# Convolution taps and six modulation pieces in the first projection, eight late pieces on GpSimd in the even attention

## What is computed

```python
mod_l = silu(c) @ w_ada[layer] + b_ada[layer]          # 6 * 1024 values; mod_c the same from c_ctx
sh1, sc1, g1, sh2, sc2, g2 = split(mod_l, 6)
h = rms_norm(x, g) * (1 + sc1) + sh1
qa, ka, va, qk_b, vb, ob, gates = split_cols(h @ w_in)
qk_b = silu(centred_conv(qk_b, conv_w, conv_b))        # 3 taps along the tokens, zero at the ends
mixed = concat([attention(qa, ka, va), mlstm_both_ways(qk_b, vb, gates) * sigmoid(ob)]) @ w_out
x = x + g1 * mixed
f = rms_norm(x, g) * (1 + sc2) + sh2                   # goes to the router and the experts
```

## Time and profile before

| | |
|---|---|
| median of the runs | 3173.81 us |
| span of the profiled execution | 3171.6 us |
| busy: PE, DVE, ACT, POOL | 2890.9, 1441.7, 1113.2, 597.7 us |
| HBM read, written | 576.73 MB, 81.66 MB |

### The profile page before, as it was taken

How to read it: one execution, slowest core, us unless ns; L and a number is a source line. 1 busy time by engine, 2 the same in 40 slices (tenths; PEclk the granted TensorE clock), 3 DMA queues, 4 the chain that set the end, 5 groups by cost and what they waited for, 6 DMA issues and landing times. The chain is left out here.

```text
span 3171.6 us, 72552 instructions
## 1 busy us (share of the span) xinstructions
PE 2890.9 (91%) x27907; PEld 1926.7 (61%) x27907; DVE 1441.7 (45%) x3981; ACT 1113.2 (35%) x2484; POOL 597.7 (19%) x825
## 2 busy tenths in 40 slices
PE   6999988899999879999996999899999959998895
PEld 3666655745544547998673455477776536775573
DVE  2333327855547642232223677666665443222223
ACT  1111114466634313333332444355553203332232
POOL 0000003500038423332230100000002003332233
...
GB/s 344 224 27 26 13 128 283 116 1 1 1 168 212 137 378 414 411 417 416 418 405 154 92 81 72 74 1 1 1 1 103 153 229 364 417 416 417 418 417 300
DMA packets 163276, 654.45 MB, mean 206 GB/s; under 512 B 24204, under 2 KB 36760, under 8 KB 113892
## 3 DMA queue, kind: packets, MB, share of 16 engines
...
HBM read 576.73 MB, written 81.66 MB: 208 GB/s over the span
## 5 line engine op out<-in xcount | busy, mean ns | idle before, releaser
L2724 PE MATMUL ps_g<-w_ring,work 128*32 128x256 f32 x7328 | 435.3, 383 | 26.1 <-DMA w_ring<-in_w 15.2
L2811 DVE STREAM_TRANSPOSE work<-work 128x256 f32<-128x256 f32 x189 | 123.5, 653 | 658.7 <-PE ps_g L2724 630.1
L2724 PEld LDWEIGHTS ps_g<-w_ring,work 128*32 128x32 f32 x7328 | 298.7, 111 | 132.0 <-issue 34.6
L2777 ACT COPY work<-ps_y 32x256 f32<-32x256 f32 x760 | 276.4, 364 | 286.1 <-PE ps_y L2739 276.9
L2724 PE MATMUL ps_g<-w_early,work 128*32 128x256 f32 x4640 | 281.0, 387 | 33.1 <-DMA w_early<-in_w 19.3
L1849 PE MATMUL of_ps_r<-w_early,cat 128*128 128x512 f32 (+1 forms) x608 | 254.9, 575 | 1.6 <-ACT cat L1931 1.6
L2724 PEld LDWEIGHTS ps_g<-w_early,work 128*32 128x32 f32 x4640 | 188.7, 112 | 103.9 <-issue 40.6
L447 PE MATMUL ps_r<-w,hT 128*128 128x512 f32 (+1 forms) x640 | 249.4, 546 | 1.5 <-ACT hT L506 1.5
L2672 POOL DMA_INDIRECT work<-f_dram,ex_idx x200 | 205.1, 1025 | 170.1 <-POOL ex_idx L2669 167.6
L2771 ACT ACTIVATE work<-ps_g 128x128 f32<-128x128 f32 x192 | 53.4, 278 | 512.4 <-PE ps_g L2724 505.8
L2739 PE MATMUL ps_y<-w_ring,work 128*32 128x256 f32 x3680 | 228.4, 382 | 3.4 <-ACT work L2777 3.4
...
## 6 DMA issues: line engine op xcount, KB each, us to landing
...
w_early<-in_w SPq DMA_DIRECT2D x152, 1024.0 KB
...
f_dram<-mo_f SPq DMA_DIRECT2D x18, 512.0 KB, 2.9
...
```

The costliest lines, as they stand in the source:

```text
L2724: mm = pe.matmul(ps_h[rows, :], xT[:, k * UNIT:(k + 1) * UNIT], w[:, :, kk * DE + n * P:kk * DE + (n + 1) * P], start=k == 0, stop=k == KD ...
L2777: w = act.copy(y[b * UNIT:(b + 1) * UNIT, n * 256:(n + 1) * 256], ps_y[n * UNIT:(n + 1) * UNIT, :])
L2811: dve.transpose(xT.rearrange("p (k t) -> p k t", k=KD), xs.rearrange("p (r k) -> p k r", k=KD)).then_inc(x_turned, 1)
```

## The change

Nothing that is computed changes; the work moves between stages.

- The taps are scaled in `modulation`. In the projection ScalarE writes each channel block as middle tap plus bias, straight from PSUM, and VectorE adds the two side taps from PSUM. The first and last column of each tile are kept raw in `L.edges`; at the start of the mLSTM four small additions join the tiles. The mLSTM's `middle` and `convolve` go.
- Six pieces (4 to 9, `SUMMED`) are worked off in tiles 1 to 6 of the projection: SyncE loads half a piece (four blocks of 128x512) at a time into the end of `zT`, which later tiles fill, VectorE multiplies and accumulates for both vectors into the end of `qT`, and SyncE stores the 128x1024 sums to `sum_dram`. In the mLSTM's front twelve loads become eight: six whole pieces, and the sums as one unit of 2 MB (four pieces) and one of 1 MB (two), each needing only a sum over partitions.
- The zero fill is four transfers from 256 columns instead of two from 512. VectorE's loop over the projection is written out from its third turn on. Two memsets move from VectorE to GpSimd, `product(2)` goes behind a matmul of the gate chain.
- The eight late pieces move into the attention: SyncE loads 64 blocks of 128x512, GpSimd scales and adds each, and SyncE stores one block per piece to `late_dram`. The mixing output loads these (2 MB) and does four matmuls and a turn for each four pieces, at tiles 2/3 and 5/6, in place of the scaling, the additions and the 64 matmuls.

The diff, cut and with its indentation taken off; each part is headed by its stage and engine.

```diff
@@ modulation, VectorE @@
+taps = lambda ap, a: ap.rearrange("p (w k) -> p w k", k=8)[:, :, a:a + 4]
+for a, scale in ((0, 0.5 * BD ** -0.5), (4, 0.5)):
+    dve.tensor_scalar(taps(L.halfw[:, :], a), taps(g.cols[:, COL_CW:COL_CW + 32], a), scale, None, ALU.mult).then_inc(*c.up())
...
@@ projection, SyncE (the loop over x goes) @@
+def x_load(n):
+    sp.wait_ge(t_done, 2 * n + 2)
+    sp.dma_start(x[:, n % 2, :], A["x"][0, n * P:(n + 1) * P, :]).then_inc(x_in[n % 2], 16)
+def slab_load(n, half):
+    if n:
+        sp.wait_ge(slab_used[half], n)
+    col = (EARLY + n) * 512
+    sp.dma_start(slabs[:, 4 * half:4 * half + 4, :],
+                 A["w_ada"][0, half * 512:(half + 1) * 512, col:col + 512].rearrange("(k p) n -> p k n", p=P)).then_inc(slab_in[half], 16)
+def acc_store(n):
+    sp.wait_ge(slab_used[1], n + 1)
+    sp.dma_start(g.sum_dram[:, n, :, :], L.qT[:, 0:2, T - 512:T]).then_inc(acc_st, 16)
+x_load(0)
+slab_load(0, 0)
+slab_load(0, 1)
+x_load(1)
+for n in range(SUMMED):
+    if n + 1 < SUMMED:
+        slab_load(n + 1, 0)
+    x_load(n + 2)
+    acc_store(n)
+    if n + 1 < SUMMED:
+        slab_load(n + 1, 1)
+for n in range(SUMMED + 2, NTL):
+    x_load(n)
...
@@ projection, GpSimd @@
-for half in range(2):
-    pool.dma_start(rows[:, :, half * 512:(half + 1) * 512],
-                   zeros[:, :].unsqueeze(1).to_broadcast([P, YB, 512])).then_inc(filled, 16)
-pool.wait_ge(filled, 32)
+for part in range(4):
+    pool.dma_start(rows[:, :, part * 256:(part + 1) * 256],
+                   zeros[:, :].unsqueeze(1).to_broadcast([P, YB, 256])).then_inc(filled, 16)
...
@@ projection, TensorE, turn_qk @@
+pe.wait_ge(z_act, i * 4 + 2 * h + 2)
...
@@ projection, ScalarE @@
 def channels_out(i, h):
-    act.wait_ge(z_done, i * 4 + 2 * h + 1)
-    act.copy(L.zT[:, 0:4, bass.ds(i * 256 + h * P, P)],
-             ps_ab[:, h, 0, :].rearrange("p (a n) -> p a n", n=P)).then_inc(z_act, 1)
+    if h == 0 and not place_of(i, h)[0] and not place_of(i, h)[1]:
+        act.wait_ge(slab_used[1], i * 2)
+    for half in range(2):
+        act.wait_ge(z_done, i * 4 + 2 * h + half + 1)
+        for cc in range(4 * half, 4 * half + 4):
+            m = act.activation(L.zT[:, cc, bass.ds(i * 256 + h * P, P)], ps_ab[:, h, half, (cc % 4) * P:(cc % 4) * P + P], ACT.Identity,
+                               scale=L.halfw[:, cc + 8:cc + 9], bias=L.halfw[:, cc + 24:cc + 25])
+        m.then_inc(z_act, 1)
...
@@ projection, VectorE @@
 def channels_out(i, h):
-    dve.wait_ge(z_done, i * 4 + 2 * h + 2)
-    dve.tensor_copy(L.zT[:, 4:8, bass.ds(i * 256 + h * P, P)],
-                    ps_ab[:, h, 1, :].rearrange("p (a n) -> p a n", n=P)).then_inc(z_dve, 1)
+    at = i * 256 + h * P
+    for half in range(2):
+        dve.wait_ge(z_act, i * 4 + 2 * h + half + 1)
+        edge = ps_ab[:, h, half, :].rearrange("p (a n) -> p a n", n=P)
+        for end, col in enumerate((0, P - 1)):
+            dve.tensor_copy(L.edges[:, end, 4 * half:4 * half + 4, bass.ds(i * 2 + h, 1)], edge[:, :, col:col + 1])
+        for cc in range(4 * half, 4 * half + 4):
+            z, raw = L.zT[:, cc, bass.ds(at + 1, P - 1)], ps_ab[:, h, half, (cc % 4) * P:(cc % 4) * P + P - 1]
+            m = dve.scalar_tensor_tensor(out=z, in0=raw, scalar=L.halfw[:, cc:cc + 1], in1=z, op0=ALU.mult, op1=ALU.add)
+        m.then_inc(*c.up())
+        dve.wait_ge(*c.now())
+        for cc in range(4 * half, 4 * half + 4):
+            z, raw = L.zT[:, cc, bass.ds(at, P - 1)], ps_ab[:, h, half, (cc % 4) * P + 1:(cc % 4) * P + P]
+            m = dve.scalar_tensor_tensor(out=z, in0=raw, scalar=L.halfw[:, cc + 16:cc + 17], in1=z, op0=ALU.mult, op1=ALU.add)
+    m.then_inc(z_dve, 1)
...
+def summed(i, h, half):
+    n = i * 2 + h - 1
+    dve.wait_ge(slab_in[half], n * 16 + 16)
+    if half == 0 and not (isinstance(n, int) and n == 0):
+        dve.wait_ge(acc_st, n * 16)
+    for k in range(4 * half, 4 * half + 4):
+        for kind in range(2):
+            by = L.cs[:, k, kind:kind + 1]
+            if k == 0:
+                m = dve.tensor_scalar(acc[kind], slabs[:, k, :], by, None, ALU.mult)
+            else:
+                dve.wait_ge(*c.but(1))
+                m = dve.scalar_tensor_tensor(out=acc[kind], in0=slabs[:, k, :], scalar=by, in1=acc[kind], op0=ALU.mult, op1=ALU.add)
+            m.then_inc(*c.up())
+    dve.wait_ge(*c.now())
+    dve.sem_inc(slab_used[half], 1)
...
+sums = not first and not (isinstance(i, int) and i * 2 + h > SUMMED)
+if sums:
+    summed(i, h, 0)
 rows_out(i, h)
 if not first:
     k_out(*before)
 norm_rope(i, h)
 if not last:
     modulate(*after)
+if sums:
+    summed(i, h, 1)
 channels_out(i, h)
 if not final:
...
@@ mLSTM @@
+units = [("sums", 0, 4), ("whole", whole), ("whole", whole + 1), ("sums", 4, SUMMED)] + [("whole", q) for q in range(whole + 2, LAST[0])]
...
@@ mLSTM, SyncE @@
 def load(n):
     if n >= len(wa):
         sp.wait_ge(ada_mm, n - len(wa) + 1)
-    ada_load(sp, A, EARLY + n, wa[buf(n)], ada_in[buf(n)])
-for n in range(6):
+    if units[n][0] == "sums":
+        _, a, b = units[n]
+        sp.dma_start(wa[buf(n)][:, 0:2 * (b - a), :], g.sum_dram[:, a:b, :, :].rearrange("p n w c -> p (n w) c")).then_inc(ada_in[buf(n)], 16)
+    else:
+        ada_load(sp, A, units[n][1], wa[buf(n)], ada_in[buf(n)])
...
@@ mLSTM, GpSimd @@
+pool.memset(tab[:, :, :], 0.0).then_inc(blank, 1)
+pool.memset(m_row[:, :, :], 0.0).then_inc(blank, 1)
+pool.memset(sel[:, :, :], 0.0).then_inc(blank, 1)
+pool.wait_ge(blank, 3)
+for kind in range(2):
+    pool.memset(sel[:, kind, kind:kind + 1], 1.0).then_inc(sel_in, 1)
 pool.memset(C[:, :, :, :], 0.0).then_inc(cleared, 1)
...
@@ mLSTM, TensorE @@
-ada_product(pe, L, ps_c[:, n % 2, :], wa[buf(n)], ada_mm)
+if units[n][0] == "sums":
+    for kind in range(2):
+        for j in range(units[n][2] - units[n][1]):
+            mm = pe.matmul(ps_c[32 * j:32 * j + 32, n % 2, :], sel[:, kind, :], wa[buf(n)][:, 2 * j + kind, :], start=kind == 0, stop=kind == 1)
+    mm.then_inc(ada_mm, 1)
+else:
+    ada_product(pe, L, ps_c[:, n % 2, :], wa[buf(n)], ada_mm)
...
-product(2)
 pe.wait_ge(gd, 3)
 pe.matmul(ps_n[:, 1, 0:1], m_row[0:1, 2, :], g.ident[0:1, 0:1], start=True, stop=True).then_inc(gp, 1)
+product(2)
...
@@ mLSTM, ScalarE @@
-def middle(cc):
-    if cc > 2:
-        act.wait_ge(z_out, cc - 2)
-    act.activation(yb[cc % 3], L.zT[:, cc, :], ACT.Identity, scale=halfw[:, cc + 8:cc + 9], bias=halfw[:, cc + 24:cc + 25]).then_inc(mid_out, 1)
 def gate(cc):
-    act.wait_ge(conv_out, cc + 1)
     if cc > 1:
         act.wait_ge(z_out, cc - 1)
-    act.activation(tb[cc % 2], yb[cc % 3], ACT.Tanh, scale=BD ** 0.5 if cc < 4 else 1.0).then_inc(t_out, 1)
-act.wait_ge(taps_in, 2)
-for cc in range(3):
-    middle(cc)
+    act.activation(tb[cc % 2], L.zT[:, cc, :], ACT.Tanh, scale=BD ** 0.5 if cc < 4 else 1.0).then_inc(t_out, 1)
+act.wait_ge(joined, 1)
+gate(0)
...
 act.activation(g_col, a_col, ACT.Ln, bias=g.ones[:, 0:1]).then_inc(gate_ln, 1)
 ada_out(0)
-gate(0)
+gate(2)
+gate(3)
 ada_out(1)
...
@@ mLSTM, VectorE @@
+for end, tap in ((0, 16), (1, 0)):
+    dve.tensor_tensor(edges[:, end, :, :], edges[:, end, :, :], halfw[:, tap:tap + 8].unsqueeze(2).to_broadcast([P, 8, NT]), ALU.mult).then_inc(*c.up())
...
-def convolve(cc):
-    y, z = yb[cc % 3], L.zT[:, cc, :]
-    dve.wait_ge(mid_out, cc + 1)
-    for a, n in ((0, CTX), (CTX, SEQ)):
-        dve.scalar_tensor_tensor(out=y[:, a + 1:a + n], in0=z[:, a:a + n - 1], scalar=halfw[:, cc:cc + 1],
-                                 in1=y[:, a + 1:a + n], op0=ALU.mult, op1=ALU.add).then_inc(*c.up())
...
-    dve.scalar_tensor_tensor(out=y[:, a:a + n - 1], in0=z[:, a + 1:a + n], scalar=halfw[:, cc + 16:cc + 17],
-                             in1=y[:, a:a + n - 1], op0=ALU.mult, op1=ALU.add).then_inc(*c.up())
-own()
...
+z4 = L.zT[:, :, :].rearrange("p a (t n) -> p a t n", n=P)
+for a, b in ((0, NTC), (NTC, NT)):
+    for end, to, of, col in ((0, slice(a, b - 1), slice(a + 1, b), P - 1), (1, slice(a + 1, b), slice(a, b - 1), 0)):
+        dve.tensor_tensor(z4[:, :, to, col], z4[:, :, to, col], edges[:, end, :, of], ALU.add).then_inc(*c.up())
...
-dve.scalar_tensor_tensor(out=L.zT[:, cc, :], in0=tb[cc % 2], scalar=1.0, in1=yb[cc % 3], op0=ALU.add, op1=ALU.mult).then_inc(z_out, 1)
+dve.scalar_tensor_tensor(out=L.zT[:, cc, :], in0=tb[cc % 2], scalar=1.0, in1=L.zT[:, cc, :], op0=ALU.add, op1=ALU.mult).then_inc(z_out, 1)
...
-dve.wait_ge(taps_in, 2)
-convolve(0)
+gated(0)
+gated(1)
...
-for cc in range(1, 8):
-    convolve(cc)
-    gated(cc - 1)
-gated(7)
+for cc in range(3, 8):
+    gated(cc)
...
@@ attention, SyncE @@
+def store(j):
+    sp.wait_ge(slab_added, (j + 1) * KD)
+    sp.dma_start(g.late_dram[:, j, :], slab[:, ((j + 1) * KD - 1) % 4, :]).then_inc(sum_st, 16)
+for n, (j, k) in enumerate(slabs):
+    if k == 3 and j:
+        store(j - 1)
+        sp.wait_ge(sum_st, 16 * j)
+    elif n >= 4:
+        sp.wait_ge(slab_added, n - 2)
```

(100 more changed lines are left out.)

107 lines of the change are left out of this document (58 added, 49 removed).

## The result

The changed kernel takes 3152.94 us (median of four runs, 3150.96 to 3157.71), before 3175.49: ratio 0.9929, 95% interval 0.9917 to 0.9941. That is 22.5 us less, 19 to 26 by the interval. Measured again beside other kernels (E5) it is 3154.9 us, ratio 0.9938 (0.9924 to 0.9952), 19.7 us less. The forecast was 3146.5. One run of E2 (3648.1 us) and one of the kernel before beside E5 to E8 (4356.8 us) were in a slow state, with mean granted clocks of 0.78 and 0.65 where all others have 0.95 to 0.96, and are left out of every median.

A forecast was written before the change was run, and what follows sets the result against it. TensorE was taken to bound projection and attention, loads the mLSTM's front. +3.5 (last turn) - 20.5 (front) - 6.5 (tail) - 7.9 (router waits) + 4.1 (added rounds) = -27.3 us, from 3173.8 to 3146.5; range 3139 to 3160.

The forecast's parts named there:

- Projection +0: Projection tiles: added taps and sums on VectorE stay hidden, with 3.9 us of slack before the transposes; 0 us.
- B: Projection: the first slab is starved by the zero fill, +24 us, total 3170; chance 0.04.
- D: Projection: VectorE's sums or the longer channel chain stall it by part of 19 us, 3150 to 3165; chance 0.07.
- The last turn +3.5: End of the projection: the last turn of q and k waits for the longer channel chain, 3.5 us more.
- Front -20.5: Front of the mLSTM, bound by loads: it ends four loads of 5.11 us earlier, -20.5 us.
- The cap of 2 to 3 us: Front of the mLSTM: had the convolution stayed there, the gain would have been capped at 2 to 3 us.
- Attention 0: Attention: the eight pieces on idle GpSimd, some 130 us against 270, stay hidden and don't slow VectorE; 0 us.
- 64 scalings at 0.61 us: Attention, GpSimd: scalings take 39 us, with 71 us of additions 110 us in all.
- rival A: Attention: GpSimd holds up VectorE's accumulating score operations, +38 us, total 3184; chance 0.05.
- Mixing output -10.3: Mixing output: -6.5 us at the tail, -7.9 for router waits and clock, +4.1 for two added rounds.
- rival C: Mixing output: router waits stay because the copy of f is late for another reason, total 3154; chance 0.08.
- The 1.7 us for a fall of the clock: Mixing output: a router wait let the clock fall, eight matmuls took 5.40 us for 3.7; 1.7 us gained.

The follow-up runs named there:

- E5: The changed kernel itself, measured again on one chip beside three other kernels, against the kernel before: 3154.9 us, ratio 0.9938.
- E2: Kernel before with only the six summed pieces moved into the projection, eight loads left, convolution still in the mLSTM: 3175.17 us, ratio 0.9996.
- E8: Changed kernel with both the last turn in the other tile's banks and pieces 12 and 13 moved into the attention: 3136.65 us, ratio 0.9877.
- E9: Changed kernel with VectorE doing the first half of each summed piece twice, eight more multiply-adds per tile on tiles 1 to 6: 3182.77 us.
- E6: Changed kernel with the last turn of q and k put into the other tile's PSUM banks: 3148.45 us.
- E1: Kernel before with only the convolution moved into the projection and the zero fill in four parts, all twelve pieces still loaded: 3179.35 us, ratio 1.0012.
- E3: Kernel before with convolution and six pieces both moved into the projection, late pieces left in the mixing output: 3159.07 us, ratio 0.9943.
- E10: Changed kernel with GpSimd in the attention scaling by an immediate 0.5 in place of the per-partition scalar: 1.49 us an operation, one run 3147.54 us.
- E7: Changed kernel with pieces 12 and 13 also moved from the mLSTM's front to GpSimd in the attention, multiplying by a broadcast tensor: 3141.56 us.
- E11: Second profile of the unchanged kernel before: 3170.57 us.
- E4: Kernel before with only the eight late pieces moved into the attention, projection and mLSTM as before: 3167.77 us, ratio 0.9974.
- E12: Third profile of the changed kernel: 3154.05 us.

## Why the prediction was right, and 5 us too far

**Projection +0: right, by its own slack.** The first half of the first piece begins at 96.68 and the copies behind it at 101.68, 5.0 us with the hand-over for the forecast 4.9. In the profile after, in the tile where VectorE's loop turns over (the one with the least slack):

```profile
219.94 0.88 DVE L671 TENSOR_SCALAR qT<-zT,cs 128x512 f32<-128x512 f32 x2 [2.71 <-issue]
...
225.53 0.29 DVE L681 COPY kT<-ps_ab 128x128 f32 x1
...
226.92 1.04 PE L467 MATMUL ps_ab<-consts_sb,x 128*128 128x128 f32 x8
```

kT is copied at 225.82, 1.1 us before the transposes are due, and these come 39.98 us after those of the tile before (186.94). In the tile before, kT is copied at 183.22, 3.7 us before the transposes, and E9 gives 3.9 us. The 2.7 us at the loop's turn were in no step of mine. The turn alone doesn't cost them: in E2, whose loop has the sums but not the side taps, VectorE begins the same tile's sums at 213.21, right behind the work before. That the longer body makes the difference is a guess. Rivals B and D are out: no tile waits, neither for a slab nor for VectorE.

**The last turn +3.5: right mechanism, 0.7 short.**

```profile
452.30 1.09 PE L507 MATMUL ps_ab<-consts_sb,sq 128*128 128x128 f32 x4 [4.13 <-DVE zT L658]
```

It waits 4.13 us for 0.88 of the earlier trace rows, 3.25 more, and after so long a wait TensorE does the four transposes in 1.09 us for 0.63. That is the 3.6 us by which this pair of profiles differs; the mean of all five says 4.2. E6 shows that the wait was for banks.

**Front -20.5: right.** In the profile after, in order of time:

```profile
455.47 0.34 SPq L809 DMA_DIRECT2D ml_staging<-sum_dram  x1
...
501.13 2.98 PE L157 MATMUL ml_ps_c<-ml_staging,cs 128*32 128x512 f32 x16 [2.63 <-DMA ml_staging<-in_w_ada]
...
502.64 0.20 POOL L875 COPY ml_cur<-ml_tab 128x16 f32<-128x16 f32 x1 [39.73 <-DMA ml_spare<-ml_rows]
```

The last load is still what TensorE and the row tables wait for, 21.9 us earlier in the mean. That both halves are needed was the claim of the prediction that E1 to E3 tested hardest, and it held. The cap of 2 to 3 us with the convolution left in place fits E2's 1.3 (-1.9 to 4.8), but in E2's profile the last gating ended at 512.7, not near 516, and the front was shorter by more than that.

**Attention 0: right in the time, wrong in GpSimd's share.** The step that failed is "64 scalings at 0.61 us": they take 1.56 us each, and GpSimd is busy 171 us, not 110. It was done 180 us into the stage's 278.6. The price came from one row of another form, with two immediates (E10).

```profile
L1286 POOL TENSOR_SCALAR ea_slab<-ea_slab,cs 128x512 f32<-128x512 f32 x64 | 99.9, 1563 | 15.9 <-DMA ea_slab<-in_w_ada 15.9
...
L1294 POOL TENSOR_TENSOR ea_slab<-ea_slab 128x512 f32<-128x512 f32 x56 | 71.3, 1273 | 4.7
...
L1425 DVE TENSOR_SCALAR_CACHE_REDUCE zT<-ea_ps_s 128x512 f32<-128x512 f32 x84 | 53.0, 687 | 12.6 <-PE ea_ps_s L1307 12.4
```

The same group of VectorE in the profile before:

```profile
L1291 DVE TENSOR_SCALAR_CACHE_REDUCE zT<-ea_ps_s 128x512 f32<-128x512 f32 x84 | 53.0, 686 | 12.6 <-PE ea_ps_s L1173 12.5
```

It takes 687 ns with GpSimd beside it and 686 without. So rival A is out. The attention of five profiles without GpSimd's work is 275.4 to 279.2 us, of nine with it 277.4 to 279.9 (E7 and E8, with more of it, 279.3); the means differ by 1.0 us, less than either group spreads.

**Mixing output -10.3: about -8.** Waits of the profile after, and then two groups of VectorE:

```profile
PE mo_ps_f L1640 <- DVE mo_f L1795: 5.4, 1, 5.4
...
PE mo_ps_r L1652 <- ACT mo_fT L1715: 3.9, 10, 0.8
```

```profile
L1792 DVE SCALAR_TENSOR_TENSOR mo_f<-zT,mo_xs,mo_rows 128x1024 f32<-128x1024 f32 x10 | 13.5, 1348 | 0.4
...
L1784 DVE TENSOR_TENSOR mo_f<-mo_ps_o,mo_rows 128x1024 f32<-128x1024 f32 x10 | 12.2, 1225 | 75.1 <-PE mo_ps_o L1630 75.1
```

Router waits fall from 9.7 us (ten, by the same window) to 3.9, 5.8 for the forecast 6.15; rival C is out. From router(8) to the last turn it is 6.1 us (1066.35 to 1072.44) for 12.7 before, and the last turn waits for f as said. The two added rounds cost 17.6 + 17.3 - 2 x 16.4 = 2.1 us each, as forecast. So between the two profiles of the table's first and third columns the stage is 9.8 us shorter, for 10.3 forecast.

What was too much came from reading one profile of before, the longest of five with the old mixing output: it took 201.7 us there and 197.4 to 201.2 in E1, E2, E3 and E11 (mean of the five 199.6), and 191.5 to 192.4 in five with the new one and two rounds (after, E4, E5, E6, E12). Two terms of the sum vary between those profiles, as the first row, of E11, and the second, of E2, show:

```profile
1084.72 10.34 PE L1561 MATMUL mo_ps_c<-consts_sb,qT 128*128 128x1 f32 x64
```

```profile
993.93 5.40 PE L1615 MATMUL mo_ps_o<-mo_w,zT 128*128 128x512 f32 x8
```

- The 64 one-column matmuls of the tail took 12.23 us in the earlier trace rows (granted clock 0.57), 12.1 in E2 (0.58), 11.1 in E3, 10.3 in E11 (0.70) and 10.1 in E1 (0.71). From router(8) to the last fold of the router it was 15.7 us in the mean, against 10.2: 5.5 us gained for the forecast 6.5.
- The 1.7 us for a fall of the clock: the eight matmuls of 5.40 us occur in three of the five (before, E2, E3; granted clock 0.72 over 6 us each time), behind router waits of 2.2, 1.9 and 1.8 us, and in none of the nine profiles with the new mixing output. The gain is real, but 1.0 us in the mean.

With the router waits (9.5 in the mean of the five, so 5.6 gained) this makes 2.2 of the 2.5 us missing.

In the profile before, the group of VectorE with an operand in PSUM was:

```profile
L1657 DVE TENSOR_TENSOR mo_f<-mo_ps_o,mo_rows 128x1024 f32<-128x1024 f32 x10 | 12.2, 1225 | 39.8 <-PE mo_ps_o L1515 39.8
```

VectorE's operation on two SBUF operands went from 2.05 to 1.35 us, the one with a PSUM operand stayed at 1.225 in both. The Trainium skill (SBUF — State Buffer, Who interferes with whom) states just this split: two SBUF inputs contend with a GpSimd instruction that reads SBUF, one does not outside the two-port modes. Here as in the attention the traces agree with it.

**The rest.** 0.9 us at the start, 2.2 in the chunk loop, 1.7 in the attention and 2.5 behind were not forecast. None is shown to come from the change; single profiles of one kernel differ by as much. The start is at 46.4 to 46.8 us in some profiles with the taps in `modulation` (E6, E7, E9, E12) and at 47.6 to 47.8 in others. In the first 20 us of the chunk loop the granted clock was 0.90 and 0.72 before, 0.69 and 0.72 after; this loop took 103.6 us in E4, where the front is unchanged. That a shorter, emptier front leaves TensorE at the lower granted clock more often is a guess that these few profiles fit and do not settle.
